# Inputs laid out transposed by the host, single first weight loads, residual steps moved, blank products first, in a two-layer decoder trunk

## The chip, the cores and the metric

The kernel runs on one core of a Trainium2 chip. The metric is device microseconds of one execution of the program on that core; lower is better. TensorE (PE in the profile) multiplies, ScalarE (ACT) and VectorE (DVE) work beside it, GpSimd (POOL) does little, and SyncE (SP) issues all DMAs.

## The reference, cut to what matters

S = 256 positions, D = 2048, two post-norm layers, float32. Layer 0 mixes tokens with a causal pooling, layer 1 with causal differential attention; in both a 4-head cross-attention into 256 memory tokens runs beside.

```python
kv = mem @ w_kv                                   # per layer: 2048 x 1024
h = x @ w_in                                      # 2048 x 2048 (pool) or 2048 x 5120 (differential)
y = jnp.concatenate([mix, mem_o], axis=-1) @ w_out[i]
x = _layernorm(DEEPNORM_ALPHA * x + y, ln1_g[i], ln1_b[i])
h = x @ w_up                                      # 2048 x 11264: gate and up halves
hc = conv_b + sum(conv_w[kk] * hp[:, kk:kk + S] for kk in range(CONV_WIDTH))
f = (jax.nn.silu(gate) * up) @ w_down             # 5632 x 2048
x = _layernorm(DEEPNORM_ALPHA * x + f, ln2_g[i], ln2_b[i])
```

## The kernel before

**Products.** Every weight matrix streams once from HBM. It is cut into chunks of 512 columns, a chunk into pieces of 512 rows (1 MB, one DMA), a piece into 4 granules of 128 rows. Each float32 operand is split into a rounded high part and the rest: ScalarE writes w_hi (`hi_granule`, L430), VectorE w_lo = raw - w_hi (`lo_granule`, L775), and TensorE makes three products, w_hi by x_hi, w_hi by x_lo and w_lo by x_hi (`product3`, L1310 to L1312). A granule is 12 products of 256 columns or 6 of 512. `raw` has four slots of one piece; SP may refill a slot once VectorE has split its piece (`slot_split`; in the differential stage, whose `tail` is set, the wait is for one piece more in three of four cases). w_hi and w_lo hold 8 granules, so ScalarE and VectorE are at most 8 granules ahead of TensorE.

**Order.** All engines run written-out programs and meet in semaphores. A position in a stage is named (n, j): piece n, granule j. The order of the stages: `s_kv` (memory keys and values of both layers, chunks 0 to 3), `s_pool_in`, `s_pool_w`, `s_out[0]`, `s_up[0]` (22 chunks in 11 pairs g: gate chunk 2g, up chunk 2g + 1), `s_down[0]`, `s_diff` (10 chunks, n = 0 to 39, with attention heads beside), `s_out[1]`, `s_up[1]`, `s_down[1]`.

**The start.** SP loads mem in token rows, interleaved with chunk 0's weights; the first piece comes as four single granules (L343). TensorE transposes mem against an identity that GpSimd makes (`ahead`, `transpose_bank`, L1373), four transposes per PSUM bank of two 128-column blocks; the first call takes banks 0 and 1. x is loaded beside chunk 1's weights and transposed in pieces n = 4 to 11 of `s_kv`, one bank per piece, between the products. `split_hi` and `split_lo` make the two parts of each bank from PSUM. After each chunk `kv_out` (L545) copies it out.

**The feed-forward pair.** While a gate chunk 2g streams (`ffn_gate`), ScalarE applies the taps of the up chunk just finished (`taps`, L529), VectorE adds the two lagging taps (`conv_bank`, L935) and multiplies with the silu. While an up chunk 2g + 1 streams (`ffn_up`), taps and silu of the gate chunk are made.

**The deferred gain and bias.** After a norm, x_tok holds the normed value without gain and bias. `resid_affine` multiplies the gain row in (L894) and adds the bias row (L897), 512 columns at a time, as a side task of the next stage. The rows lie in the one buffer `gb`. SP's `load_rows` waits until the step before has freed it, and stands in SP's program like this:

```python
with nc.sync.Fori(0, 4) as g:
    load_pair(g)              # 8 pieces: chunks 2g and 2g + 1
    load_rows(l, 0, 2 * l, g) # waits for resid_affine(g - 1, 1)
```

In pairs 1 to 4 VectorE does step (g - 1, 0) after piece 2 of the chunk 2g + 1 and step (g - 1, 1) two granules later. In the differential stage the steps for c stand at (n % 4, j) = (2, 2) and (3, 2) of the chunk after c, and `load_rows(c)` behind the four pieces of chunk c.

## Time and profile before

| | |
|---|---|
| median of three runs | 2241.58 us (2238.80 to 2241.73) |
| the profiled execution, its own time | 2234.63 us |
| its span, first to last instruction | 2232.9 us |
| TensorE busy | 97% of the span |
| mean granted clock | 0.99 |
| DMA, 10 to 20 us and 20 to 30 us | 393 and 387 GB/s |
| issue of SP's second load (the first weight granule) | 1.25 us |
| w_lo of one granule on VectorE (L775), mean | 685 ns |
| VectorE's first residual sum into x_tok (L820) | 241.02 us |

Times in rows are microseconds from the span's start. Products are pipelined: each shows a longer duration than the distance to the next, so TensorE's pace is read from starts, and a wait of TensorE is an idle time in brackets with what ended it. The clock column reads 1.00 in the first ten microseconds, where the starts of the products are what tells the clock. "L775" is line 775 of the kernel.

### The profile page before, as it was taken

The page shows a single profiled execution, that of the slowest core. Times are in us where ns is not written, and L with a number is a line of the kernel's source. Part 1 is how long each engine was busy: PE and PEld are TensorE (multiplying, and loading weights), DVE is VectorE, ACT ScalarE, POOL GpSimd, SP SyncE. Part 2 cuts the span into 40 slices and gives each one's busy share as a digit, 9 for nine tenths or more (in the row PEclk, how much of TensorE's full clock was granted, in tenths as well). Part 3 has the DMA queues.
Part 4 walks back from the last instruction along what each step waited for, and adds up shares of the span by engine and source line. Part 5 has one row for each costly group of instructions (what it writes and reads, how often), then busy time and mean ns, then how long its engine had stood idle before and what let it go on. Part 6 is the DMA issues. An engine that isn't in the chain of part 4 may idle for free.

```text
span 2232.9 us, 39246 instructions
## 1 busy us (share of the span) xinstructions
PE 2175.7 (97%) x14328; PEld 1973.4 (88%) x14328; DVE 1368.6 (61%) x2456; ACT 1124.5 (50%) x2112; POOL 9.4 (0%) x15
## 2 busy tenths in 40 slices
PE   8999999999999999999999999999999999999996
PEld 8999889999999998888777777889999999988885
DVE  5557666666756575455656557566767666665555
ACT  5545555545555454444545556465545455544442
POOL 0000000000000000000000000000000000000001
PEclk9999999999999999999999999999999999999998
DMA  8555545456555555555444454544555555465552
GB/s 312 171 177 167 200 159 180 160 171 242 183 193 182 194 173 185 188 190 187 142 170 160 151 171 154 203 161 163 200 204 175 194 175 196 153 242 207 188 188 75
DMA packets 204510, 406.65 MB, mean 182 GB/s; under 512 B 7696, under 2 KB 9744, under 8 KB 203920
## 3 DMA queue, kind: packets, MB, share of 16 engines
q1 hardware_dynamic: 204432, 405.61, 52.8%
q8 instruction: 49, 0.80, 0.1%
q14 instruction: 29, 0.24, 0.0%
HBM read 402.44 MB, written 3.15 MB: 182 GB/s over the span
## 4 chain that ended last, share of the span: by engine, by line
PE 88%; DVE 5%; DMA 3%; ACT 2%; issue 2%; SPq 0%; DVEq 0%; ACTq 0%
PE acc L1310 28%; PE acc L1311 28%; PE acc L1312 28%; DMA raw<-in_ffn_w_up 2%; DVE w_lo L775 2%; PE acc L1373 1%; ACT w_hi L430 1%; DMA raw<-in_diff_w_in 1%; DVE conv L935 1%; PE acc L1542 0%; DVE x_tok L897 0%; PE acc L1516 0%; DVE x_tok L894 0%; PE acc L1437 0%; DVE x_tok L1282 0%
## 5 line engine op out<-in xcount | busy, mean ns | idle before, releaser
L775 DVE TENSOR_TENSOR w_lo<-raw,w_hi 128x512 fp32r<-128x512 f32 x1484 | 961.0, 685 | 504.0 <-ACT w_hi L430 501.1
L430 ACT ACTIVATE w_hi<-raw 128x512 fp32r<-128x512 f32 x1480 | 864.6, 627 | 558.8 <-PE acc L1312 472.9
L1310 PE MATMUL acc<-ffn_xT,w_hi 128*128 128x256 f32 x3072 | 865.8, 282 | 11.0 <-DVE w_lo L775 10.8
L1311 PE MATMUL acc<-ffn_xT,w_hi 128*128 128x256 f32 x3072 | 862.2, 281 | 0.0
L1312 PE MATMUL acc<-ffn_xT,w_lo 128*128 128x256 f32 x3072 | 862.1, 281 | 0.0
L1310 PEld LDWEIGHTS acc<-ffn_xT,w_hi 128*128 128x128 f32 x3072 | 580.2, 189 | 13.1 <-DVE w_lo L775 12.0
L1311 PEld LDWEIGHTS acc<-ffn_xT,w_hi 128*128 128x128 f32 x3072 | 580.2, 189 | 0.2
L1312 PEld LDWEIGHTS acc<-ffn_xT,w_lo 128*128 128x128 f32 x3072 | 580.1, 189 | 0.0
L935 DVE SCALAR_TENSOR_TENSOR conv<-acc,table,conv 128x255 f32<-128x255 f32 (+1 forms) x352 | 153.3, 477 | 224.4 <-ACT conv L529 211.8
L1310 PE MATMUL acc<-w_hi,ffn_act 128*128 128x512 f32 x704 | 279.1, 397 | 0.0
L1311 PE MATMUL acc<-w_lo,ffn_act 128*128 128x512 f32 x704 | 278.4, 395 | 0.0
L1312 PE MATMUL acc<-w_hi,ffn_act 128*128 128x512 f32 x704 | 276.7, 393 | 0.0
L1310 PE MATMUL acc<-w_hi,ffn_xT 128*128 128x512 f32 x576 | 235.8, 409 | 1.6 <-DVE w_lo L775 0.8
L1312 PE MATMUL acc<-w_hi,ffn_xT 128*128 128x512 f32 x576 | 228.2, 396 | 0.0
L1311 PE MATMUL acc<-w_lo,ffn_xT 128*128 128x512 f32 x576 | 227.8, 395 | 0.0
L529 ACT ACTIVATE conv<-acc,table 128x256 f32<-128x256 f32 x176 | 84.8, 562 | 195.9 <-PE acc L1312 195.9
L1312 PEld LDWEIGHTS acc<-w_hi,ffn_act 128*128 128x128 f32 x704 | 132.2, 188 | 32.9
L1310 PEld LDWEIGHTS acc<-w_hi,ffn_act 128*128 128x128 f32 x704 | 132.1, 188 | 32.2
L1311 PEld LDWEIGHTS acc<-w_lo,ffn_act 128*128 128x128 f32 x704 | 132.1, 188 | 31.1
L1312 PEld LDWEIGHTS acc<-w_hi,ffn_xT 128*128 128x128 f32 x576 | 108.7, 189 | 27.1
L1310 PEld LDWEIGHTS acc<-w_hi,ffn_xT 128*128 128x128 f32 x576 | 109.1, 189 | 26.1 <-DVE ffn_xT L797 1.6
L1311 PEld LDWEIGHTS acc<-w_lo,ffn_xT 128*128 128x128 f32 x576 | 109.1, 189 | 23.3
(177 smaller groups left out, 1058.9 us busy)
## 6 DMA issues: line engine op xcount, KB each, us to landing
raw<-in_ffn_w_up SPq DMA_DIRECT2D x176, 1024.0 KB, 4.9
raw<-in_ffn_w_down SPq DMA_DIRECT2D x88, 1024.0 KB, 5.1
raw<-in_diff_w_in SPq DMA_DIRECT2D x40, 1024.0 KB, 5.5
raw<-in_w_out SPq DMA_DIRECT2D x32, 1024.0 KB, 5.1
raw<-in_pool_w_in SPq DMA_DIRECT2D x16, 1024.0 KB, 5.2
raw<-in_mem_w_kv SPq DMA_DIRECT2D x15, 1024.0 KB, 8.8
gb<-in_ln_g SPq DMA_DIRECT2D x12, 256.0 KB, 4.3
gb<-in_ln_b SPq DMA_DIRECT2D x12, 256.0 KB, 6.3
```

The lines of the kernel that those rows point to most:

```text
L430: nc.scalar.activation(w_hi[:, st.split_at(k, j), 0:st.width], raw[:, k % SLOTS, j * CHUNK:j * CHUNK + st.width], ACT.Copy).then_inc(hi_ma ...
L529: ins = nc.scalar.activation(conv[:, s, b, f * S:(f + 1) * S], acc[:, 2 * s + b, f * S:(f + 1) * S], ACT.Identity, bias=table[:, l, bass.d ...
L775: nc.vector.tensor_tensor(w_lo[:, at, 0:st.width], raw[:, k % SLOTS, j * CHUNK:j * CHUNK + st.width], w_hi[:, at, 0:st.width].bitcast(F32) ...
L935: ins = nc.vector.scalar_tensor_tensor(to, acc[:, 2 * s + b, f * S:(f + 1) * S - lag], table[:, l, bass.ds(col, 1)], to, ALU.mult, ALU.add)
L1310: pe.matmul(out, w[0], x[0], start=start, stop=False, skip_group_check=True)
L1311: pe.matmul(out, w[0], x[1], start=False, stop=False, skip_group_check=True)
L1312: return pe.matmul(out, w[1], x[0], start=False, stop=stop, skip_group_check=True)
L1373: ins = pe.transpose(acc[:, b, f * S + t * P:f * S + (t + 1) * P], src[:, t, (kt + f) * P:(kt + f + 1) * P], ident[:, :])
```

## The change

The host passes x and mem also as x_T and mem_T, 128 rows of [16 blocks, 256 positions]. SP loads mem_T in seven parts (`MEM_PARTS`: 1, 1, 2, 2, 2, 4, 4 blocks) between the weights of chunk 0, whose first two pieces come as eight single granules with a semaphore each; x_T comes in four parts beside chunk 1. ScalarE and VectorE split both from SBUF (`mem_hi`, `x_hi`, `mem_lo`, `x_lo`), x in pieces 8 to 15 of `s_kv` and no longer 4 to 12; TensorE's 16 banks of transposes go. x_tok is still needed later and gets a 2 MB load of its own behind the memory weights of layer 1. VectorE clears a tile, and TensorE makes eight blank 128-column products of it at the very start. The residual steps move: in the feed-forward pairs from the last two pieces of chunk 2g + 1 to piece 1 of the gate chunk 2g; in the differential stage one piece earlier, and there `load_rows(c)` now stands ahead of piece 3 of chunk c.

```diff
+MEM_PARTS = ((0, 1), (1, 2), (2, 4), (4, 6), (6, 8), (8, 12), (12, 16))
+SINGLES = 2 * PIECE
...
-        return (c * self.uses[s] + (self.loads[s] + k // SLOTS + 1)) * 16
+        return (c * self.uses[s] + (self.loads[s] + k // SLOTS + 1) - (1 if s < SINGLES // PIECE else 0)) * 16
...
-        for c, (name, to, loaded) in enumerate((("mem", mem_tok, mem_loaded), ("x", x_tok, x_loaded))):
-            src = a[name][0].rearrange("(t p) n -> p t n", p=P)
-            for k in range(4):
-                cs = slice(k * CHUNK, (k + 1) * CHUNK)
-                if c > 0 or k > 0:
-                    sp.dma_start(to[:, :, cs], src[:, :, cs]).then_inc(loaded[k], 16)
-                    load_piece(s_kv, c, k, a["mem_w_kv"][0], c * CHUNK)
-                    continue
-
-                half = CHUNK // 2
-                sp.dma_start(to[:, :, 0:half], src[:, :, 0:half]).then_inc(mem_half_loaded, 16)
-                for j in range(PIECE):
-                    sp.dma_start(raw[:, 0, j * CHUNK:(j + 1) * CHUNK], a["mem_w_kv"][0][j * P:(j + 1) * P, 0:CHUNK]).then_inc(
-                        granule_loaded[j] if j < PIECE - 1 else piece_loaded[0], 16)
-                    if j == 0:
-                        sp.dma_start(to[:, :, half:CHUNK], src[:, :, half:CHUNK]).then_inc(loaded[0], 16)
+        def load_mem(i):
+            lo, hi = MEM_PARTS[i]
+            sp.dma_start(mem_raw[:, lo:hi, :], a["mem_T"][:, lo:hi, :]).then_inc(mem_loaded[i], 16)
+
+        def load_single(i):
+            j = i % PIECE
+            sp.dma_start(raw[:, i // PIECE, j * CHUNK:(j + 1) * CHUNK], a["mem_w_kv"][0][i * P:(i + 1) * P, 0:CHUNK]).then_inc(
+                granule_loaded[i], 16)
+
+        for i in range(SINGLES):
+            if i in (0, 1, 2, 4, 6):
+                load_mem((0, 1, 2, 4, 6).index(i))
+            load_single(i)
+        for k in range(2, 4):
+            load_mem(3 + k)
+            load_piece(s_kv, 0, k, a["mem_w_kv"][0], 0)
+        for k in range(4):
+            load_piece(s_kv, 1, k, a["mem_w_kv"][0], CHUNK)
+            sp.dma_start(x_raw[:, 4 * k:4 * k + 4, :], a["x_T"][:, 4 * k:4 * k + 4, :]).then_inc(x_loaded[k], 16)
...
+        sp.dma_start(x_tok[:, :, :], a["x"][0].rearrange("(t p) n -> p t n", p=P)).then_inc(x_tok_loaded, 16)
...
-                    load_chunk(s_diff, c, a["diff_w_in"][0], DIFF_ORDER[c] * CHUNK, OUT_PIECES[1] if c == DIFF_LAST else None)
+                    for k in range(4):
+                        load_piece(s_diff, c, k, a["diff_w_in"][0], DIFF_ORDER[c] * CHUNK, OUT_PIECES[1][k] if c == DIFF_LAST else None)
+                        if k == 2 and c < 4:
+                            load_rows(0, 1, 1, c)
                     if c == 0:
                         sp.wait_ge(kv1_stored, 16)
                         sp.wait_ge(granule_used, s_down[0].used(3))
                         sp.dma_start(kv1[:, :, :], kv1_dram[:, :, :]).then_inc(kv1_loaded, 16)
-                    if c < 4:
-                        load_rows(0, 1, 1, c)
...
+        def mem_hi(lo, hi):
+            for part, loaded in zip(MEM_PARTS, mem_loaded):
+                if part[0] == lo:
+                    act_e.wait_ge(loaded, 16)
+            nc.scalar.activation(memT[:, lo:hi, 0, :], mem_raw[:, lo:hi, :], ACT.Copy).then_inc(hi_split["mem"], 1)
+
+        def x_hi(b):
+            if b % 2 == 0:
+                act_e.wait_ge(x_loaded[b // 2], 16)
+            nc.scalar.activation(xT[:, 2 * b:2 * b + 2, 0, :], x_raw[:, 2 * b:2 * b + 2, :], ACT.Copy).then_inc(hi_split["x"], 1)
+
+        for n in range(16):
             c, k = n // 4, n % 4
             for j in range(PIECE):
-                hi_granule(s_kv, c, k, j)
-                if c == 0 and j in (0, 2):
-                    b = 2 * k + j // 2
-                    split_hi("mem", b, memT, 2 * b, acc[:, 4 + b % 4, :])
-                if 5 <= n < 13 and j == 1:
-                    split_hi("x", n - 5, xT, 2 * (n - 5), acc[:, 4 + (n - 5) % 4, :])
+                i = PIECE * n + j
+                if i < 2:
+                    mem_hi(i, i + 1)
+                elif i < KT and i % 2 == 0:
+                    mem_hi(i, i + 2)
+                if i < SINGLES:
+
+                    act_e.wait_ge(granule_loaded[i], 16)
+                    nc.scalar.activation(w_hi[:, s_kv.split_at(k, j), :], raw[:, k, j * CHUNK:(j + 1) * CHUNK], ACT.Copy).then_inc(hi_made, 1)
+                else:
+                    hi_granule(s_kv, c, k, j)
+                if 8 <= n and j == 1:
+                    x_hi(n - 8)
...
+        nc.vector.memset(conv[:, 0, 0, 0:P], 0.0).then_inc(blank_made, 1)
...
+        def mem_lo(lo, hi):
+            dve.wait_ge(hi_split["mem"], lo + 1 if lo < 2 else lo // 2 + 2)
+            nc.vector.tensor_tensor(memT[:, lo:hi, 1, :], mem_raw[:, lo:hi, :], memT[:, lo:hi, 0, :].bitcast(F32),
+                                    ALU.subtract).then_inc(split["mem"], 1)
+
+        def x_lo(b):
+            dve.wait_ge(hi_split["x"], b + 1)
+            kts = slice(2 * b, 2 * b + 2)
+            nc.vector.tensor_tensor(xT[:, kts, 1, :], x_raw[:, kts, :], xT[:, kts, 0, :].bitcast(F32), ALU.subtract).then_inc(split["x"], 1)
+
+        for n in range(16):
             c, k = n // 4, n % 4
             for j in range(PIECE):
+                i = PIECE * n + j
+                if i < 2:
+                    mem_lo(i, i + 1)
+                elif i < KT and i % 2 == 0:
+                    mem_lo(i, i + 2)
                 lo_granule(s_kv, c, k, j)
-                if c == 0 and j in (0, 2):
-                    b = 2 * k + j // 2
-                    split_lo("mem", b, memT, 2 * b, acc[:, 4 + b % 4, :])
-                if 5 <= n < 13 and j == 1:
-                    split_lo("x", n - 5, xT, 2 * (n - 5), acc[:, 4 + (n - 5) % 4, :])
+                if 8 <= n and j == 1:
+                    x_lo(n - 8)
...
+                dve.wait_ge(x_tok_loaded, 16)
...
-                    if c < 4 and n % 4 >= 2 and j == 2:
-                        resid_affine(0, 1, 1, c, n % 2)
+                    if c < 4 and n % 4 in (1, 2) and j == 2:
+                        resid_affine(0, 1, 1, c, n % 4 - 1)
...
-            def ffn_gate(g):
+            def ffn_gate(g, resid):
                 lo_piece(s_up[l], 2 * g, 0)
                 conv_bank(l, 1, 0, g - 1)
-                lo_piece(s_up[l], 2 * g, 1)
+                lo_granule(s_up[l], 2 * g, 1, 0)
+                if resid:
+                    resid_affine(l, 0, 2 * l, g - 1, 0)
+                lo_granule(s_up[l], 2 * g, 1, 1)
+                lo_granule(s_up[l], 2 * g, 1, 2)
+                if resid:
+                    resid_affine(l, 0, 2 * l, g - 1, 1)
+                lo_granule(s_up[l], 2 * g, 1, 3)
                 conv_bank(l, 1, 1, g - 1)
                 product(l, 0, g - 1)
                 lo_piece(s_up[l], 2 * g, 2)
@@ -1239,24 +1275,17 @@
                 lo_piece(s_up[l], 2 * g, 3)
                 act_lo_part(l, 1, g - 1)
 
-            def ffn_up(g, resid=False):
+            def ffn_up(g):
                 lo_piece(s_up[l], 2 * g + 1, 0)
                 conv_bank(l, 0, 0, g)
                 lo_piece(s_up[l], 2 * g + 1, 1)
                 conv_bank(l, 0, 1, g)
                 lo_piece(s_up[l], 2 * g + 1, 2)
-                if resid:
-                    resid_affine(l, 0, 2 * l, g - 1, 0)
-                lo_granule(s_up[l], 2 * g + 1, 3, 0)
-                lo_granule(s_up[l], 2 * g + 1, 3, 1)
-                if resid:
-                    resid_affine(l, 0, 2 * l, g - 1, 1)
-                lo_granule(s_up[l], 2 * g + 1, 3, 2)
-                lo_granule(s_up[l], 2 * g + 1, 3, 3)
+                lo_piece(s_up[l], 2 * g + 1, 3)
 
             def ffn_pair(g, resid):
-                ffn_gate(g)
-                ffn_up(g, resid)
+                ffn_gate(g, resid)
+                ffn_up(g)
...
-        pe.wait_ge(ident_made, 2)
+        pe.wait_ge(blank_made, 1)
+        for _ in range(8):
+            pe.matmul(acc[:, 7, 0:P], conv[:, 0, 0, 0:P], conv[:, 0, 0, 0:P], start=True, stop=True)
 
         for n in range(16):
             c, k = n // 4, n % 4
             if c >= 2 and k == 0:
                 pe.wait_ge(kv_evacuated, c - 1)
-            if 4 <= n < 12:
-                b = n - 4
-                pe.wait_ge(x_loaded[b // 2], 16)
-                if b < 4:
-                    pe.wait_ge(split["mem"], 5 + b)
-                else:
-                    pe.wait_ge(split["x"], b - 3)
-                transpose_bank("x", b, 4 + b % 4, x_tok, 2 * b)
             for j in range(PIECE):
-                if c == 0 and j % 2 == 0:
-                    ahead("mem", 2 * k + j // 2, mem_tok, lambda b: pe.wait_ge(mem_loaded[b // 2] if b > 0 else mem_half_loaded, 16))
+                i = PIECE * n + j
+                if i < 2:
+                    pe.wait_ge(split["mem"], i + 1)
+                elif i < KT and i % 2 == 0:
+                    pe.wait_ge(split["mem"], i // 2 + 2)
...
+    for name in ("x", "mem"):
+        laid_out[f"{name}_T"] = np.asarray(inputs[name])[0].reshape(S, KT, P).transpose(2, 1, 0)
```

## Rows read from the trace of the kernel before

**Rows 1.** The page's chain that ended last: share of each engine
```profile
PE 88%; DVE 5%; DMA 3%; ACT 2%; issue 2%; SPq 0%; DVEq 0%; ACTq 0%
```

**Rows 2.** Timeline of ScalarE, chunk copies: start us, us, engine line; idle before, releaser
```profile
34.21 1.02 ACT L545 ACTIVATE memory_kv<-acc 128x1024 f32<-128x1024 f32 x1 [5.00 <-PE acc L1312]
...
58.38 1.03 ACT L545 ACTIVATE memory_kv<-acc 128x1024 f32<-128x1024 f32 x1 [3.97 <-PE acc L1312]
...
83.06 1.03 ACT L545 ACTIVATE memory_kv<-acc 128x1024 f32<-128x1024 f32 x1 [4.06 <-PE acc L1312]
...
105.46 1.03 ACT L545 ACTIVATE memory_kv<-acc 128x1024 f32<-128x1024 f32 x1 [4.97 <-PE acc L1312]
```

**Rows 3.** Timeline of TensorE, the first products
```profile
7.64 0.56 PE L1310 MATMUL acc<-memory_memT,w_hi 128*128 128x256 f32 x1
8.00 0.42 PE L1311 MATMUL acc<-memory_memT,w_hi 128*128 128x256 f32 x1
8.21 0.41 PE L1312 MATMUL acc<-memory_memT,w_lo 128*128 128x256 f32 x1
...
9.68 0.28 PE L1310 MATMUL acc<-memory_memT,w_hi 128*128 128x256 f32 x1
```

**Rows 4.** Chain that ended last, first 140 us: start us, us, what
```profile
1.76 5.06 DMA memory_mem<-in_mem
...
34.17 0.44 PE acc L1373 x4
```

**Rows 5.** One source line: the single first weight loads, L343
```profile
DMA to landing us min/median/max: 4.1/5.3/5.5
```

**Rows 6.** TensorE's waits, 390-560, then 1535-1660 us: total, times, longest
```profile
PE acc L1310 <- DVE w_lo L775: 5.5, 3, 1.8
...
PE acc L1310 <- DVE w_lo L775: 5.3, 3, 2.0
```

**Rows 7.** Timeline of ScalarE: taps, first work after a feed-forward chunk's end
```profile
387.06 1.47 ACT L529 ACTIVATE conv<-acc,table 128x256 f32<-128x256 f32 x3 [5.29 <-PE acc L1312]
...
532.29 1.02 ACT L529 ACTIVATE conv<-acc,table 128x256 f32<-128x256 f32 x2 [5.21 <-PE acc L1312]
...
577.35 1.48 ACT L529 ACTIVATE conv<-acc,table 128x256 f32<-128x256 f32 x3 [5.21 <-PE acc L1312]
...
1533.28 1.47 ACT L529 ACTIVATE conv<-acc,table 128x256 f32<-128x256 f32 x3 [5.21 <-PE acc L1312]
...
1675.60 1.93 ACT L529 ACTIVATE conv<-acc,table 128x256 f32<-128x256 f32 x4 [5.21 <-PE acc L1312]
```

**Rows 8.** Chain that ended last, 300-830 us, around the first stall
```profile
399.05 1.17 DVE x_tok L897
...
401.77 8.14 DMA raw<-in_ffn_w_up
```

**Rows 9.** Windows: busy of each engine, PEclk (granted), DMA share, GB/s
```profile
508.00:510.00 2.00, 2.00 (x11) 2.00 (x11) 1.90 (x5) 2.00 (x5) 0.00 (x0) 0.50 1.05 384
```

**Rows 10.** Timeline of VectorE, one gate chunk and one up chunk
```profile
372.16 2.69 DVE L775 TENSOR_TENSOR w_lo<-raw,w_hi 128x512 fp32r<-128x512 f32 x4
...
396.65 1.21 DVE L894 TENSOR_TENSOR x_tok<-x_tok,gb 128x1024 f32 x1
397.79 1.28 DVE L775 TENSOR_TENSOR w_lo<-raw,w_hi 128x512 fp32r<-128x512 f32 x2
```

**Rows 11.** Timeline of TensorE, first product of that gate's ninth granule
```profile
375.24 0.28 PE L1310 MATMUL acc<-ffn_xT,w_hi 128*128 128x256 f32 x1
```

**Rows 12.** Timeline of TensorE, its three waits in the differential projection
```profile
1129.79 0.50 PE L1310 MATMUL acc<-w_hi,ffn_xT 128*128 128x512 f32 x1 [0.79 <-DVE w_lo L775]
...
1162.06 1.22 PE L1437 MATMUL acc<-diff_probs,diff_kv 128*128 128x256 f32 x2 [4.47 <-ACT diff_probs L494]
...
1193.85 0.39 PE L1542 MATMUL acc<-diff_qkT 64*128 64x128 f32 x2 [1.00 <-ACT diff_scores L655]
```

**Rows 13.** Timeline of VectorE, the residual add before the longest of them
```profile
1149.21 1.22 DVE L897 TENSOR_TENSOR x_tok<-x_tok,gb 128x1024 f32<-128x1024 f32 x1
```

More of the change, by code:

```diff
@@ L208, in build @@
     xT, act = region("ffn", [split_x, ("act", [P, FF_T, 2, S], F32R)])
-    _, kvbuf, qmT0, memT, mem_tok = region("memory", [
+    _, kvbuf, qmT0, memT, mem_raw, x_raw = region("memory", [
         split_x, ("kv", [P, 8, 512], F32), ("qmT", [P, MEM_HEADS, S], F32), ("memT", [P, KT, 2, S], F32R),
-        ("mem", [P, TT, D], F32)])
+        ("mem", [P, KT, S], F32), ("x", [P, KT, S], F32)])
     _, _, _, dT, pool_h, pool_a, pool_b, probs0 = region("pool", [
@@ L250, in build @@
     s_out, s_up, s_down = (s_out0, s_out1), (s_up0, s_up1), (s_down0, s_down1)
-    mem_half_loaded, granule_loaded = sem("mem_half_loaded"), [sem(f"granule_loaded{j}") for j in range(PIECE - 1)]
+    granule_loaded = [sem(f"granule_loaded{i}") for i in range(SINGLES)]
     piece_loaded = [sem(f"piece_loaded{s}") for s in range(SLOTS)]
@@ L256, in build @@
     granule_used = sem("granule_used")
-    x_loaded = [sem(f"x_loaded{c}") for c in range(4)]
-    mem_loaded = [sem(f"mem_loaded{c}") for c in range(4)]
+    mem_loaded = [sem(f"mem_loaded{i}") for i in range(len(MEM_PARTS))]
+    x_loaded, x_tok_loaded = [sem(f"x_loaded{i}") for i in range(4)], sem("x_tok_loaded")
     table_loaded, small_loaded = sem("table_loaded"), sem("small_loaded")
     zeroed, ident_made, steps_made, pads_made = sem("zeroed"), sem("ident_made"), sem("steps_made"), sem("pads_made")
-    rounded = sem("rounded")
+    rounded, blank_made = sem("rounded"), sem("blank_made")
     pool_evacuated, pool_diffed, dT_hi, dT_made = sem("pool_evacuated"), sem("pool_diffed"), sem("dT_hi"), sem("dT_made")
@@ L993, in sine_arguments @@
             nc.vector.tensor_scalar(trig[:, 2, :, :], part, -1.0, math.pi / 2, ALU.mult, ALU.add).then_inc(trig_arg, 1)
-        split_lo("mem", 0, memT, 0, acc[:, 4, :])
-        lo_granule(s_kv, 0, 0, 0)
-        split_lo("mem", 1, memT, 2, acc[:, 5, :])
-        for j in range(1, PIECE):
-            lo_granule(s_kv, 0, 0, j)
-        for n in range(1, 16):
+        def mem_lo(lo, hi):
[7 more added lines that the diff above has]
+        for n in range(16):
             c, k = n // 4, n % 4
             for j in range(PIECE):
-                lo_granule(s_kv, c, k, j)
-                if c == 0 and j in (0, 2):
-                    b = 2 * k + j // 2
-                    split_lo("mem", b, memT, 2 * b, acc[:, 4 + b % 4, :])
-                if 5 <= n < 13 and j == 1:
-                    split_lo("x", n - 5, xT, 2 * (n - 5), acc[:, 4 + (n - 5) % 4, :])
+                i = PIECE * n + j
[3 more added lines that the diff above has]
+                    mem_lo(i, i + 2)
+                lo_granule(s_kv, c, k, j)
+                if 8 <= n and j == 1:
+                    x_lo(n - 8)
                 if (n, j) == (13, 3):
@@ L1374, in transpose_bank @@
             ins.then_inc(banked[stage], 1)
-        def ahead(stage, i, src, need):
-            for b in ((0, 1), (2, 3))[i] if i < 2 else (i + 2,):
-                if b < KT // 2:
-                    need(b)
-                    if b >= 4:
-                        pe.wait_ge(split[stage], b - 3)
-                    transpose_bank(stage, b, 4 + b % 4, src, 2 * b)
-            pe.wait_ge(split[stage], i + 1)
         def normed_ahead(l, n, kt):
@@ L1410, in mem_beside @@
                         if l == 0:
+                            pe.wait_ge(ident_made, 2)
                             pe.wait_ge(qm_evacuated, 1)
@@ L1628, in build @@
     ctx.close()
-_INS = ["table", "x", "mem", "positions", "pool_w_in", "pool_w", "diff_w_in", "diff_lambda_q1", "diff_lambda_k1",
+_INS = ["table", "x", "x_T", "mem_T", "positions", "pool_w_in", "pool_w", "diff_w_in", "diff_lambda_q1", "diff_lambda_k1",
         "diff_lambda_q2", "diff_lambda_k2", "diff_subln_g", "mem_w_kv", "w_out", "ln1_g", "ln1_b", "ffn_w_up",
```

7 lines of the change are left out of this document (removed).

## The prediction

> **What bounds the kernel now.** I began with the chain that ended last: TensorE holds 88% of it [rows 1]. So only two things shorten this kernel: less TensorE work, or fewer stretches in which it stands still or runs at half clock. The work itself has a floor that can be read off: ScalarE copies each finished chunk of the first projection out, and chunks 2 to 3 ended 105.46 - 83.06 = 22.40 us apart [rows 2]. That is 16 granules (a granule is one 128-row slab of weights) at 1.40 us. In the feed-forward network one pair of chunks without a gap takes 577.35 - 532.29 = 45.06 us [rows 7]. Every stage is held against these figures; what is above them is what a change can give back.
>
> Three places stand above the floor where the diff works. **The start:** chunk 0 ends at 34.21 instead of 22.4 us after the first product, and chunks 1 and 2 take 24.17 and 24.68 [rows 2]. **The feed-forward pairs 1 to 4:** TensorE waits three times in each layer for w_lo, 5.5 and 5.3 us in sum [rows 6]. **The memory and score part of the differential projection:** three waits of 0.79, 4.47 and 1.00 us [rows 12].
>
> The feed-forward waits have one cause, to be read backwards in the chain [rows 8]: TensorE waits for w_lo, that for a weight load of 8.14 us, and that was issued late because SP stood at `load_rows`, which waits for the residual add L897. SP issues in order. It asks for gain row g right after pair g's last piece, while VectorE sends the signal only in the last piece of that pair; the slots of the next chunk are long free, but nobody fills them.
>
> **The change, part by part.**
>
> 1. *Transposes out.* x needs 8 banks, mem 8 banks, four transposes each, 0.44 us on TensorE's path per bank [rows 4]. The x banks sit four in chunk 1 and four in chunk 2: 4 x 0.44 = 1.76 us each, which is just chunk 1's 24.17 - 22.40 = 1.77. Sum 3.5 us. The copies on ScalarE and VectorE stay, with an SBUF source; same size, taken at the same price, and hidden by the several granules that these engines are ahead there.
>
> 2. *The first chunk.* Now the first product starts at 7.64 [rows 3], because the second mem load landed only at 1.76 + 5.06 = 6.82 [rows 4] and its transposes stood in TensorE's queue ahead of it. Afterwards granule 0 needs a 128 KB mem part and one 256 KB weight load. The single weight loads landed 4.1 to 5.5 us after issue [rows 5]; issued second, at 1.25 as before (the table), that is 5.35, and less if the smaller load ahead helps; plus a split of about 0.6 and 0.7 on the two engines: 6.3 to 6.8. So 0.8 to 1.3 us earlier. Chunk 0 then took 34.0 - 7.64 = 26.4 us. Over 22.4 that is 4.0: the six later mem banks (6 x 0.44 = 2.6) and the products at half clock. Those start 0.21 apart instead of 0.117 (22.40 / 192) until 9.68 [rows 3], about 1 us lost. I keep that 1 us. Against it: can the loads keep up? Chunk 0 needs 6 MB for mem and weights. At the 390 GB/s of the table the last 1 MB piece is in after about 21 us, and granule 12, which needs it, is due at about 24; piece 2 (granule 8) is in at about 17 to 18 and due at 18 to 19. It is tight there, so I charge 0.7. Chunk 0 ends at 6.5 + 22.4 + 1.0 + 0.7 = 30.6: 3.4 to 3.6 us earlier (bounds: 2 if granules 1 to 8 come one by one late, 5 if the half clock goes too). With part 1: 7.1 us.
>
> The blank products fill TensorE before any data is there. The row shows that before, the full rate came at 9.68, after the transposes and two us of products. The Trainium skill ("TensorE: Matmul & The Clock Gate", Part 1) says that activity releases the clock, so the blanks might bring that forward. By the rule the start would be worth up to 1 us more, but the loads bound the same stretch, so by the row it is nothing; I take nothing.
>
> 3. *x_tok loaded a second time.* 2 MB on SP's queue behind the second layer's memory weights: some 5.4 us of transfer at 390 GB/s, once, while three pieces (3 x 5.6 us of TensorE) are ahead. VectorE first sums into it at 241 us (the table), during the output projection. Nothing.
>
> 4. *Feed-forward: residual steps to the gate chunk's second piece.* The signal for gain row g now comes in pair g's piece 1, before SP has issued the pair's last piece, so `load_rows` finds it there and the three stalls of each layer go. What they cost: from chunk 3's start to chunk 9's TensorE takes 532.29 - 387.06 = 145.23 us in layer 0, 10.05 above 3 x 45.06; in layer 1 1675.60 - 1533.28 = 142.32, 7.14 above [rows 7]. That holds the waits and what followed (the clock fell to 0.50 behind one, [rows 9]). Gain 17.2 us.
>  What it costs: two instructions, which hold VectorE 397.79 - 396.65 = 1.14 us [rows 10], two 2.28 us, now in piece 1 of the gate chunk; the tightest granule behind them is the first of piece 2. Its w_lo begins at 372.16 [rows 10], takes 0.69 (the page's mean, 685 ns), and TensorE uses it at 375.24 [rows 11]: 2.39 us to spare. The move eats 2.28. It fits by a hair, at eight gates; I charge 0.1 us in all (bounds: 0, and 8 x 1 us if the conv steps beside it stretch). Behind it the products, `act_lo` and the up chunk have more room.
>
> 5. *Differential projection: residual one piece earlier, gain rows before piece 3.* This looks like the same cure and isn't. SP asks for row c ahead of piece 3 of chunk c; the signal comes in piece 2 of the same chunk. So SP still stands until VectorE is there, and then it is piece 3, not the next chunk's piece 0, which is late, with the same two granules and the same lead to cover some 8 us of load. Stall one: before 0.79; after, by the same sum, about 1. Stall two: VectorE ended L897 at 1149.21 + 1.22 = 1150.4 [rows 13]; TensorE ran dry 7.2 us later (1162.06 - 4.47 = 1157.6) and resumed at 1162.06 [rows 12], 11.6 after L897: gain rows asked for, 8 us of load, the copies and the head's exp behind it on ScalarE. After, the same 11.6 us hits the head before it, and L894 now runs in that head's stretch on VectorE, so the 7.2 shrink by up to 1.14: 4.5 to 5.6 us. Stall three: piece 3 lands before the first scores, saves up to 1.0. And the multiply L894 now stands at VectorE between head maxima that TensorE waits for: up to 1.14. Sum 0.8 us slower (bounds: 8 us faster if the lead does cover the load, as below; 6 slower if a stall doubles).
>
> **Sum**, against the profiled execution's own 2234.63 us (span 2232.9 and 1.7 around it): -7.1 - 17.2 + 0.8 + 0.1 = -23.4, so 2211.2. The median of the plain runs is 2241.58, 7 us above that execution, so the forecast for the median is 2241.6 - 23.4 = 2218.2; 2218.
>
> **The rivals**, in the median's terms.
>
> A. *The start is bound by its loads.* The first eight weight loads are 256 KB, each with its own way to landing; if they feed TensorE more slowly than 1.4 us a granule, the removed transposes turn into waits for w_lo in chunk 0, and only 3.5 + 0.5 us of part 1 and 2 are left: 2221. For it: even 256 KB took 4.1 to 5.5 us [rows 5]. Against: they overlap. The Trainium skill ("DMA: Bandwidth & Descriptors", Rules for kernel authors) asks for 1 MiB or more per load for full bandwidth; this rival is what that rule would do here. Chance 0.13.
>
> B. *The differential stage gets clearly worse.* Piece 3's late load meets the memory head chain with less lead and a second stretch at half clock: 6 us more, 2224. For it: one such wait already cost 4.47 [rows 12]. Chance 0.15.
>
> C. *The differential stage is relieved.* VectorE reaches piece 2 when TensorE is still nine granules behind (12.6 us), so the load is covered: 0.79 + 4.47 + 1.00 = 6.3 go, and half clock behind the long one, an estimate of 2 from [rows 9], which shows 1.0 lost in 2 us; with my 0.8 that is 9 us: 2209. Chance 0.12.
>
> D. *The feed-forward stalls stay*, because SP still reaches `load_rows` before the signal: then only the start is won, 2235. Against: between the two places lie some six pieces of VectorE's work. Chance 0.03.
>
> E. *Slower.* The one mechanism is the gate: the 2.28 us lie where TensorE's chunk end, the taps and the conv steps run in series. Were nothing to spare, each of eight gates would lose 2.28 us and, as in [rows 9], 1.0 of half clock: 26 us, 2244. It decides from 23.5 / 8 = 2.9 us per gate on. Against: 2.39 to spare [rows 10, 11]. Chance 0.03.
>
> My forecast holds 0.54. Range 2210 to 2228: it takes in A and B with their neighbours and the 5-us bound of the start, and leaves C's core, D and E outside. Some 0.2 % (4.5 us) is what a measurement of this kernel can tell from no change; faster by more 0.95, within it 0.02, slower 0.03.
>
> **What would show it.** The chunk copies (now L545) at about 30.8, 53.2, 75.6 and 98.0; no wait of TensorE for w_lo in the pairs 1 to 4 and even chunks of 22.5 us; SP's `load_rows` no longer followed by loads issued in a burst there, but still so in the differential stage, with one long TensorE wait near a memory head. Waits for w_lo at each gate's ninth granule would speak for E. The forecast fails if the stalls of the pairs reappear elsewhere, above all in the differential stage, where the sum rests on leads of a few us.

## The result and the profile after

The changed kernel takes 2216.67 us (median of 4 runs, 2215.53 to 2217.42), the kernel before, beside it on the same chip, 2240.19 us (4 runs, 2237.16 to 2241.73). The ratio is 0.9896, with a 95% interval of 0.9879 to 0.9913: 23.5 us faster. The forecast was 2218.0. The profiled execution after took 2216.79 us (span 2215.0), 17.8 less than the profiled one of before; e1 and e9 below bear on why the two differences are unequal.

The page's chain, share of each engine, answers [rows 1]: less DVE and DMA, so less of the end hangs on late weights.

```profile
PE 92%; DVE 4%; DMA 2%; ACT 1%; issue 1%; SPq 0%; DVEq 0%; ACTq 0%
```

ScalarE's timeline, the chunk copies and then the taps, answers [rows 2] and [rows 7].

```profile
30.63 1.03 ACT L554 ACTIVATE memory_kv<-acc 128x1024 f32<-128x1024 f32 x1 [3.38 <-PE acc L1341]
53.02 1.02 ACT L554 ACTIVATE memory_kv<-acc 128x1024 f32<-128x1024 f32 x1 [4.96 <-PE acc L1341]
75.80 1.03 ACT L554 ACTIVATE memory_kv<-acc 128x1024 f32<-128x1024 f32 x1 [5.06 <-PE acc L1341]
98.20 1.02 ACT L554 ACTIVATE memory_kv<-acc 128x1024 f32<-128x1024 f32 x1 [4.96 <-PE acc L1341]
...
380.52 1.93 ACT L538 ACTIVATE conv<-acc,table 128x256 f32<-128x256 f32 x4 [5.28 <-PE acc L1341]
...
516.35 1.93 ACT L538 ACTIVATE conv<-acc,table 128x256 f32<-128x256 f32 x4 [5.21 <-PE acc L1341]
...
1521.46 1.93 ACT L538 ACTIVATE conv<-acc,table 128x256 f32<-128x256 f32 x4 [5.21 <-PE acc L1341]
...
1657.81 1.94 ACT L538 ACTIVATE conv<-acc,table 128x256 f32<-128x256 f32 x4 [5.21 <-PE acc L1341]
```

The four copies stand within 0.2 us of the forecast 30.8, 53.2, 75.6 and 98.0. By the last one the start gave 105.46 - 98.20 = 7.3 us. The same six chunks of the feed-forward network take 516.35 - 380.52 = 135.83 and 1657.81 - 1521.46 = 136.35 us, where [rows 7] gave 145.23 and 142.32: 15.4 us less. Three pairs without a gap would be 135.2.

TensorE's timeline, four stretches: the start, the gate's ninth granule, and the differential projection. It answers [rows 3], [rows 11] and [rows 12].

```profile
5.82 0.36 PE L1339 MATMUL acc<-memory_memT,w_hi 128*128 128x256 f32 x1 [1.16 <-DVE w_lo L795]
6.02 0.28 PE L1340 MATMUL acc<-memory_memT,w_hi 128*128 128x256 f32 x1
6.14 0.28 PE L1341 MATMUL acc<-memory_memT,w_lo 128*128 128x256 f32 x1
...
8.02 0.36 PE L1339 MATMUL acc<-memory_memT,w_hi 128*128 128x256 f32 x1 [0.54 <-DVE w_lo L795]
...
9.90 0.36 PE L1339 MATMUL acc<-memory_memT,w_hi 128*128 128x256 f32 x1 [0.21 <-DVE w_lo L795]
...
18.96 0.35 PE L1339 MATMUL acc<-memory_memT,w_hi 128*128 128x256 f32 x1 [0.36 <-DVE w_lo L795]
...
368.43 0.28 PE L1341 MATMUL acc<-ffn_xT,w_lo 128*128 128x256 f32 x1
368.61 0.39 PE L1339 MATMUL acc<-ffn_xT,w_hi 128*128 128x256 f32 x1
...
1109.38 0.50 PE L1339 MATMUL acc<-w_hi,ffn_xT 128*128 128x512 f32 x1 [2.59 <-DVE w_lo L795]
...
1142.64 2.07 PE L1457 MATMUL acc<-diff_probs,diff_kv 128*128 128x256 f32 x4 [5.67 <-ACT diff_probs L503]
```

Three things are to be seen. The first product starts at 5.82 instead of 7.64, and from the second on they are 0.12 apart: full rate from the start, in this execution; under e8 are others. Granules 0, 1, 2 and 8 of chunk 0 now wait for their weights. And two waits of the differential projection grew: 0.79 became 2.59, 4.47 became 5.67; the third, of 1.00, is gone.

VectorE's timeline in that gate chunk, with both residual steps (L914, L917), and then the residual steps of the differential projection, answers [rows 10] and [rows 13].

```profile
361.38 1.22 DVE L914 TENSOR_TENSOR x_tok<-x_tok,gb 128x1024 f32 x1
...
363.72 1.22 DVE L917 TENSOR_TENSOR x_tok<-x_tok,gb 128x1024 f32 x1
...
367.86 2.69 DVE L795 TENSOR_TENSOR w_lo<-raw,w_hi 128x512 fp32r<-128x512 f32 x4
...
1096.09 1.22 DVE L917 TENSOR_TENSOR x_tok<-x_tok,gb 128x1024 f32<-128x1024 f32 x1
...
1129.37 1.22 DVE L917 TENSOR_TENSOR x_tok<-x_tok,gb 128x1024 f32<-128x1024 f32 x1
```

The ninth granule's w_lo begins at 367.86 and is ready 0.69 later, at 368.55; TensorE takes it at 368.61, 0.18 after the product ahead of it where the pace is 0.12. The slack of 2.39 us is used up to nothing, and the product comes 0.06 us late. Over all eight gates the distances around the ninth granule add up to 0.8 us above the pace.

SP's timeline in the differential projection: both gain-row loads (L333), then weights.

```profile
1097.34 0.34 SPq L333 DMA_DIRECT2D gb<-in_ln_g  x1
1097.72 0.43 SPq L333 DMA_DIRECT2D gb<-in_ln_b  x1
1098.20 13.33 SPq L323 DMA_DIRECT2D raw<-in_diff_w_in  x4
...
1130.61 0.34 SPq L333 DMA_DIRECT2D gb<-in_ln_g  x1
1131.00 0.43 SPq L333 DMA_DIRECT2D gb<-in_ln_b  x1
1131.47 13.67 SPq L323 DMA_DIRECT2D raw<-in_diff_w_in  x4
```

Both times the rows are asked for right as L917 ends (1096.09 + 1.22 = 1097.31, 1129.37 + 1.22 = 1130.59): SP had stood there. The chain of the same stretch gives the loads behind them:

```profile
1098.20 9.75 DMA raw<-in_diff_w_in
...
1131.47 8.27 DMA raw<-in_diff_w_in
```

### The profile page after: what moved, and what is told of

Read it like the earlier page. It is cut to its first block, busy times and chain, and to the rows that moved or that the text cites. A ratio compares the mean times of both kernels' runs of the same rounds, so it can differ in the third digit from the quotient of the medians.

```text
span 2215.0 us, 39167 instructions
## 1 busy us (share of the span) xinstructions
PE 2169.3 (98%) x14280; PEld 1967.5 (89%) x14280; DVE 1371.5 (62%) x2458; ACT 1127.3 (51%) x2113; POOL 9.4 (0%) x15
## 4 chain that ended last, share of the span: by engine, by line
PE 92%; DVE 4%; DMA 2%; ACT 1%; issue 1%; SPq 0%; DVEq 0%; ACTq 0%
PE acc L1339 30%; PE acc L1341 30%; PE acc L1340 30%; DVE w_lo L795 1%; DMA raw<-in_diff_w_in 1%; PE acc L1402 1%; DMA raw<-in_mem_w_kv 0%; ACT w_hi L439 0%; PE acc L1533 0%; PE acc L1559 0%; DVE x_tok L1311 0%; PE acc L1457 0%; DVE stats L859 0%; DVE x_tok L858 0%; PE acc L1563 0%
## 5 line engine op out<-in xcount | busy, mean ns | idle before, releaser
L439 ACT ACTIVATE w_hi<-raw 128x512 fp32r<-128x512 f32 (+1 forms) x1476 | 862.5, 627 | 502.3 <-PE acc L1341 472.1
## 6 DMA issues: line engine op xcount, KB each, us to landing
raw<-in_mem_w_kv SPq DMA_DIRECT2D x14, 1024.0 KB, 10.6
```

The costliest lines, as they stand in the source:

```text
L439: nc.scalar.activation(w_hi[:, st.split_at(k, j), 0:st.width], raw[:, k % SLOTS, j * CHUNK:j * CHUNK + st.width], ACT.Copy).then_inc(hi_ma ...
```

## The experiments

Each was timed with the kernel before beside it on the same chip; each ratio is to that.

**e1. The kernel before, profiled and timed once more**, with no edit.

> The kernel before, unchanged, profiled a second time. Its first profiled execution took 2234.63 us, 5.6 us under its median of 2240.19, while the changed kernel's took 2216.79, 0.1 over its median. Theory (clock): the stalls of the old kernel sometimes cost an extra stretch at half clock and sometimes not, depending on where in time they fall; then this trace shows the same waits of TensorE within 0.2 us each, but other stretches at a clock of 0.50, and its time lies 3 to 7 us above the first profiled one. Rival (waits): the waits themselves are longer in other executions; then the waits for w_lo in the feed-forward pairs sum to well over 5.5 and 5.3 us.

Measured: 2237.06 us, ratio 0.9999 (0.9984 to 1.0013). The waits are there again (its table of waits):

```profile
PE acc L1310 <- DVE w_lo L775: 11.6, 7, 2.1
...
PE acc L1437 <- ACT diff_probs L494: 4.6, 1, 4.6
```

But the half clock behind the feed-forward stalls is not. One window of this run, then one of the profile of before, each around the end of the first stall (the number behind the five engines' is the granted clock, then come DMA share and GB/s):

```profile
410.00:418.00 8.00, 7.58 (x64) 7.58 (x65) 7.60 (x16) 6.14 (x13) 0.00 (x0) 1.00 1.03 373
```

```profile
412.00:416.00 4.00, 4.00 (x23) 4.00 (x22) 3.75 (x8) 4.00 (x10) 0.00 (x0) 0.57 1.05 386
```

The taps at 386.10 and 528.47 put layer 0's six chunks at 142.37 us here against 145.23 in [rows 7]. So some 3 us of the 17.2 that the forecast read off one execution were clock stretches that come in some executions and not in others. How long TensorE waited does not decide it: in layer 0 the three waits were 1.84, 1.81 and 1.80 us in the profile of before, with half clock behind the first and the last, and 2.06, 2.06 and 1.52 us here, with none. Yet this profiled execution took 2237.35 us, 2.7 more than the first; that is the slower pace of some chunks, told under e6 and e9.

**e2. The feed-forward part alone** in the kernel before: the residual steps in piece 1 of the gate chunk.

> Only the feed-forward part of the change on the kernel before. Theory of the prediction: SP's wait at the gain rows goes, and with it three stalls a layer; by chunk starts the two traces differ by 9.4 us in layer 0 and 5.8 us in layer 1, so the trace shows 15 us; the plain runs 15 to 21 us, if the clock stretches behind the stalls are more frequent than in the profiled execution. Rival (gate): the move is paid by waits at the ninth granule of the gate chunks; then each of the eight gates shows more than 0.3 us. Rival (start): most of the 23.5 us comes from the start; then this is under 12 us.

Measured: 2223.71 us, ratio 0.9937 (0.9922 to 0.9952), which is 14.1 us (10.7 to 17.5), a little below the 15 to 21 expected. No stall for w_lo of the kind of [rows 6] is left. The feed-forward step is most of the gain.

**e3. The start alone**: inputs transposed by the host, single loads, blanks.

> Only the start of the change (inputs laid out transposed, eight single weight loads, blank products) on the kernel before; feed-forward and differential stage as before. Theory: 7.2 us faster, constant over the executions (7 to 8), since no stall there is left to chance. Rival: over 12 us, if the missing 5.7 us between the medians and the two profiles come from the start.

Measured: 2228.84 us, ratio 0.9957 (0.9940 to 0.9974): 9.6 us (5.8 to 13.4). In the trace TensorE begins the first product of `s_pool_in` 7.0 us earlier, and the feed-forward stalls stand as before (5.4 us in three waits in layer 0). Here the first products ran at half clock in spite of the blanks (e8).

**e4. The differential part alone**: residual steps one piece earlier, `load_rows` ahead of piece 3.

> Only the differential stage's part: residual steps one piece earlier, gain rows asked for ahead of piece 3. Prediction: 0.8 us slower; by the two traces 3.7 us slower (chunks 1 and 2 together +4.9, chunks 3 and 4 -1.4). Theory: the wait for the gain rows is only moved ahead of piece 3; 2 to 5 us slower than before. Rival: the loss in the trace is the clock's chance and the part is neutral, within 1 us of before.

Measured: 2237.34 us over 12 runs, ratio 1.0003 (0.9992 to 1.0013): nothing, at most 3 us either way. TensorE's timeline has the two waits again, 0.73 and 5.28:

```profile
1124.54 0.50 PE L1311 MATMUL acc<-w_hi,ffn_xT 128*128 128x512 f32 x1 [0.73 <-DVE w_lo L776]
...
1155.86 2.07 PE L1438 MATMUL acc<-diff_probs,diff_kv 128*128 128x256 f32 x4 [5.28 <-ACT diff_probs L495]
```

**e7. The changed kernel with before's differential projection.**

> The changed kernel with the differential stage as in the kernel before. By the traces of the changed kernel and the one before that part costs 3.7 us; the part alone on the kernel before was within 1 us of it in the plain runs and 1.3 us slower in its trace. Theory: 1 to 4 us faster than the changed kernel. Rival: no difference, under 0.5 us, the 3.7 us being chance of the clock.

Measured: 2216.84 us, ratio 0.9903 (0.9886 to 0.9921), beside 0.9896 for the whole change. So in neither surrounding can the runs tell this part from nothing. From the first product of that stage to the first of its sixth chunk TensorE took 144.40 us here, 148.97 in the trace of the whole change, 145.30 before and 145.60 in e4; the 3.7 that the profile after lost there are not what the plain runs lose. Two more traces have the same edit in that stage: 144.96 us in e8 and 147.35 in e12. So one edit gives 145.0 to 149.0 us, and what the kernel before has there gives 144.4 to 146.0 in seven traces.

**e5. The rows asked for a chunk later.** In the changed kernel, the differential residual steps go back to where they were, and SP asks for the rows of c behind piece 2 of chunk c + 1:

```diff
-                        if k == 2 and c < 4:
-                            load_rows(0, 1, 1, c)
+                        if k == 2 and 1 <= c < 5:
+                            load_rows(0, 1, 1, c - 1)
...
-                    if c < 4 and n % 4 in (1, 2) and j == 2:
-                        resid_affine(0, 1, 1, c, n % 4 - 1)
+                    if c < 4 and n % 4 >= 2 and j == 2:
+                        resid_affine(0, 1, 1, c, n % 2)
```

> The changed kernel, but in the differential stage the residual steps stand where they stood before, and SP asks for gain row c only behind piece 2 of chunk c + 1, by which time VectorE's signal is there. Theory: what is lost in that stage is SP standing still in front of free slots; then TensorE's waits of 2.6 (w_lo in chunk 1), 5.7 (the memory head) and about 1 us (chunk 3) go and so do the two half-clock stretches of 3.4 and 6.8 us behind the first two (1.7 and 3.4 us): chunks 0 to 4 of the stage take 135 to 139 us instead of 149, and the kernel is 10 to 14 us faster than the changed one. Rival: the head chains set the pace there anyway; then under 4 us.

Measured: 2206.29 us, ratio 0.9847 (0.9831 to 0.9863); its median is 10.4 us below the changed kernel's. From e7 it differs in SP's request alone, and it is 10.6 us below e7, timed on the same chip beside the same runs of before; the two intervals are far apart. From the first product of the stage to that of its sixth chunk TensorE took 135.16 us, as the theory had it. One window of 95 us over the stage's first four chunks, this kernel first, the changed kernel below it:

```profile
1085.00:1180.00 95.00, 95.00 (x450) 76.44 (x449) 57.65 (x117) 50.13 (x110) 0.00 (x0) 1.00 0.54 177
```

```profile
1095.00:1190.00 95.00, 86.74 (x394) 69.03 (x392) 48.47 (x103) 42.88 (x97) 0.00 (x0) 0.95 0.48 161
```

TensorE is busy all 95 us at full clock, where the changed kernel leaves 8.3 idle and has 0.95 of the clock. Together with e7 this shows the cause that the forecast named: where SP's request stands relative to VectorE's signal.

**e10. The feed-forward stalls cured on SP's side alone.** In the kernel before, the residual steps unmoved:

```diff
-            with nc.sync.Fori(0, 4) as g:
-                load_pair(g)
-                load_rows(l, 0, 2 * l, g)
+            load_pair(0)
+            with nc.sync.Fori(1, 5) as g:
+                load_chunk(s_up[l], 2 * g, a["ffn_w_up"][l], g * CHUNK)
+                load_rows(l, 0, 2 * l, g - 1)
+                load_chunk(s_up[l], 2 * g + 1, a["ffn_w_up"][l], g * CHUNK + D_FF)
```

> The kernel before, with one edit: in the feed-forward stage SP issues the gain and skip rows of the next gate pair one gate chunk later; the residual steps themselves stay where they were. Theory that SP's waiting behind the residual step is the whole cause of the feed-forward stalls: all of e2's gain, 14 us (2223 to 2226 us, ratio 0.9925 to 0.995), with no wait of the ninth piece in the gate chunks. Rival (VectorE's place of the residual step counts for itself): under half of it, 2231 us or more, and the stalls of 4 to 6 us behind each gate pair stay in the trace.

Measured: 2217.46 us, ratio 0.9921 (0.9900 to 0.9941): 17.7 us (13.2 to 22.3), all of e2's; the intervals overlap. The excess need not be the edit's: no chunk of this trace runs at the slower pace told below, 34 of e2's do, and 34 x 0.26 = 8.7 us is most of the 9.7 by which the two profiled executions differ. The one wait for w_lo left in the whole run (its table of waits) is in the differential projection:

```profile
PE acc L1312 <- DVE w_lo L777: 0.9, 1, 0.9
```

No product at a gate's ninth granule is late either. SP's waiting is the whole cause of those stalls; VectorE's place plays no part of its own, and the gate need not be touched.

**e6 and e9. Both stages together**: e5, and the feed-forward residual steps in and behind the gate chunk's piece 3; SP's feed-forward request stays where it was. e9 is the same kernel again.

> As the run before it, and in the feed-forward pairs the two residual steps stand in and behind piece 3 of the gate chunk instead of in piece 1. Theory: the short waits at the ninth granule of eight gate chunks (0.05 to 0.15 us each in the changed kernel's trace) go; 0.5 to 1.2 us in sum. A second theory, from the traces of this study: products of 256 columns run in one of two paces, 22.53 or 22.78 us a feed-forward chunk, and the pace is taken anew at a wait of TensorE; then with no wait in a feed-forward stage all 21 chunks of a layer have the same pace, fast or slow. Rival: the pace changes in mid-stage without a wait.

> The kernel of e6 once more, unchanged, to look again at its trace. Theory of the two paces: its time is 2199.9 us plus 5.5 us for each layer's up-projection (21 chunks of 256-column products) that runs at the slow pace. A profile near 2199.9 has none of the 42 chunks slow, one near 2205.4 has 21, one near 2211 has all 42, and the mean of a chunk is 22.53 or 22.78 us with hardly anything between. Rival (the spread comes from transfers or from the clock): a profile near 2205.4 has its 5.5 us in stalls or in a stretch at half clock, with as few slow chunks as that of e6. Ratio to the kernel before 0.985 either way.

Measured: 2205.48 us, ratio 0.9848 (0.9830 to 0.9865), and 2200.34 us, ratio 0.9843 (0.9820 to 0.9866). The nine runs lie in two groups, five at 2199.73 to 2200.59 and four at 2205.44 to 2205.90, with nothing between. Both profiles were of the lower group, so the waits and the pace of an upper one were not seen. What a pace is, two timelines of ScalarE show, this kernel's (e9) and e8's, taps four chunks apart in a stretch in which TensorE is never idle:

```profile
559.16 1.93 ACT L538 ACTIVATE conv<-acc,table 128x256 f32<-128x256 f32 x4 [5.21 <-PE acc L1341]
...
649.26 1.93 ACT L538 ACTIVATE conv<-acc,table 128x256 f32<-128x256 f32 x4 [5.21 <-PE acc L1341]
```

```profile
563.15 1.93 ACT L538 ACTIVATE conv<-acc,table 128x256 f32<-128x256 f32 x4 [5.27 <-PE acc L1340]
...
654.28 1.93 ACT L538 ACTIVATE conv<-acc,table 128x256 f32<-128x256 f32 x4 [5.27 <-PE acc L1340]
```

That is 90.10 against 91.13 us for four chunks (768 products), 0.26 a chunk. Windows of both over 560 to 650 us read busy throughout and the same granted clock:

```profile
560.00:650.00 90.00, 90.00 (x769) 90.00 (x768) 58.31 (x104) 47.78 (x89) 0.00 (x0) 1.00 0.56 186
```

```profile
560.00:650.00 90.00, 90.00 (x761) 90.00 (x760) 58.38 (x104) 47.89 (x88) 0.00 (x0) 1.00 0.56 185
```

The 21 chunks of one layer after the first would be 21 x 0.255 = 5.4 us, the distance of the two groups. This fits and is not shown for them. For the two profiled executions of before the traces have it: in the six chunks with the stalls e1 took 2.9 us less in layer 0 and 0.4 less in layer 1, and among the other chunks it had 26 slow ones against 2, 24 x 0.255 = 6.1 us more (an estimate). The sum, 2.8, is near the 2.7 between them.

**e8. The changed kernel without the blanks.**

> The changed kernel without the blank products. In its trace the first real products start 0.12 us apart, at full clock, where those of the kernel before started 0.21 apart until 9.68 us. Theory (the prediction's): the loads bound the first granules (TensorE waits for w_lo at granules 1, 2 and 8), so the half clock is hidden and this is under 0.7 us slower. Rival (clock rule): the blanks bring the clock up, and without them 1 to 2 us are lost, chunk 0 ending at 31.5 or later instead of 30.4.

Measured: 2220.37 us, ratio 0.9903 (0.9886 to 0.9920), not told apart from the changed kernel's by the runs. TensorE's timeline has the first product at 5.81 and starts 0.21 apart until 11.50:

```profile
6.38 0.41 PE L1340 MATMUL acc<-memory_memT,w_lo 128*128 128x256 f32 x1
6.59 0.41 PE L1338 MATMUL acc<-memory_memT,w_hi 128*128 128x256 f32 x1
```

Chunk 1's first product comes at 31.20, 0.77 us later than in the profile after. That is not the price of the blanks, for the traces with the same start and the same blanks differ among themselves. The products were 0.12 apart from the second on in the profile after, e5 and e12; they were 0.21 apart until 10.35 in e3, 9.12 in e6, 9.70 in e7 and 9.10 in e9. TensorE's timeline of e9:

```profile
5.77 0.55 PE L1339 MATMUL acc<-memory_memT,w_hi 128*128 128x256 f32 x1 [0.93 <-DVE w_lo L795]
6.13 0.42 PE L1340 MATMUL acc<-memory_memT,w_hi 128*128 128x256 f32 x1
6.34 0.41 PE L1341 MATMUL acc<-memory_memT,w_lo 128*128 128x256 f32 x1
```

Chunk 1 began at 30.43 and 30.37 in the profile after and e5 (full rate), and at 30.65, 30.46, 31.18 and 30.75 in e3, e6, e7 and e9 (half clock). So half clock at the start costs 0 to 0.8 us here, and whether the blanks save any of it is not shown; in e8, without them, it lasted longest.

**e11. The blanks alone** in the kernel before.

> The kernel before with the eight blank matmuls put ahead and nothing else. Theory (the blanks warm the clock for the first products and do no more): 0.5 to 1.2 us faster, ratio 0.9995, the first products 0.12 us apart from their start at about 7.6 us, where before they were 0.21 to 0.23 apart; as the loads bound this chunk's end too, up to half of it may be lost again in waits for pieces. Rival (the blanks delay the first transposes or the weight load): first product at 8 us or later and no gain. The interval of the ratio will hold 1 either way, so the trace decides.

Measured: 2235.14 us over 12 runs, ratio 0.9991 (0.9976 to 1.0007), and in its trace the theory does not hold. TensorE's timeline from the end of the blanks, which run from 1.06 us:

```profile
4.63 1.06 PE L1374 MATMUL acc<-ident,memory_mem 128*128 128x128 f32 x4
6.42 1.12 PE L1374 MATMUL acc<-ident,memory_mem 128*128 128x128 f32 x4 [0.72 <-DMA memory_mem<-in_mem]
7.80 0.55 PE L1311 MATMUL acc<-memory_memT,w_hi 128*128 128x256 f32 x1 [0.26 <-DVE w_lo L775]
...
9.64 0.41 PE L1313 MATMUL acc<-memory_memT,w_lo 128*128 128x256 f32 x1
9.86 0.31 PE L1311 MATMUL acc<-memory_memT,w_hi 128*128 128x256 f32 x1
```

The first products are 0.21 apart until 9.86, later than the 9.68 of [rows 3]. In this execution the blanks brought nothing. The transposes and 0.98 us of idle time between them and the first product need not be the reason: with no work in between, four of the seven traces under e8 had half clock too. What decides is open.

**e12. Four single loads instead of eight** in the changed kernel, with the mem parts of blocks 4 to 7 ahead of the 1 MB piece 1:

```diff
-SINGLES = 2 * PIECE
+SINGLES = PIECE
...
-            if i in (0, 1, 2, 4, 6):
-                load_mem((0, 1, 2, 4, 6).index(i))
+            if i in (0, 1, 2):
+                load_mem((0, 1, 2).index(i))
...
+        load_mem(3)
+        load_mem(4)
+        load_piece(s_kv, 0, 1, a["mem_w_kv"][0], 0)
```

> The changed kernel, with the first four weight pieces alone loaded one by one as now but the rest of chunk 0 and the memory tokens' last two parts in another order: the memory parts go ahead of the 1 MB piece 1. Theory (the start is bound by the bytes that must land before the last product of chunk 0, whatever their order): chunk 1 starts within 0.5 us of the changed kernel's 30.43 us and the ratio stays at 0.9896. Rival (the order of these loads holds the start back): chunk 1 starts 1 us or more away from it, earlier if the memory parts were late, later if the pieces were.

Measured: 2219.93 us, ratio 0.9926 (0.9906 to 0.9947). TensorE starts as early, but the next piece's first granule is 2.50 us late, and chunk 1 begins 2.7 us later:

```profile
15.97 0.36 PE L1342 MATMUL acc<-memory_memT,w_hi 128*128 128x256 f32 x1 [2.50 <-DVE w_lo L798]
```

My theory, that only the sum of the bytes counts, fell: how soon the second piece's first granule lands counts. Size and order of the loads were changed together, so the 2.7 us are the price of both, and neither has been priced alone.

## Why the prediction was right, term by term

**Start, -7.1.** It held: 7.3 in the profile, and 7.0 in e3's. Inside, a pair of errors cancelled. The forecast kept 1 us of half clock and charged 0.7 for the loads. In the profile after the half clock was gone, and in its place came waits for weights, 0.54 + 0.21 + 0.36 = 1.1 us behind the first product. (The 1.16 before it is no loss against the forecast: it came at 5.82, ahead of the 6.3 to 6.8.) In e3 the half clock stayed and TensorE waited for no weights in chunk 0, and chunk 1 began 0.2 us later. So the forecast's reason for taking nothing for the blanks, that the loads bound the same stretch, was right. The Trainium skill ("TensorE: Matmul & The Clock Gate", Part 1) says that activity releases the clock; of the seven traces with this start and the blanks, three agree at the first product and four show full rate only at 9.1 to 10.4 us. Part 1's 3.5 is in the copies, 22.39 and 22.78 apart. The single loads landed in

```profile
DMA to landing us min/median/max: 3.1/6.0/6.6
```

against [rows 5]; that granules of 256 KB come one after the other just ahead of TensorE is rival A's mechanism at a small price. The Trainium skill ("DMA: Bandwidth & Descriptors", Rules for kernel authors) asks for 1 MiB or more per load for full bandwidth. e12 puts a 1 MB load where four singles stood and loses 2.7 us; at a start, where the first landing counts, that speaks against the rule, though the order of the loads was changed with it.

**x_tok's second load, nothing.** No wait for it; the waits for transposes behind the norms are 13.7 us in three before and after.

**Feed-forward, -17.2 and +0.1.** The mechanism was right and the size too large: 15.4 in the profiles, 14.1 alone (10.7 to 17.5). Two parts of the excess can be read. Some 3 us of the 145.23 were clock stretches that e1 had not. And 135.83 + 136.35 is 1.8 above the 270.4 of six gapless pairs. Of that 0.4 is the gates in them, where the slack forecast at a hair was a hair short (0.8 over all eight gates): the 0.1 for all eight was too small but right in kind, and rival E, which needed 2.9 us a gate to decide, was far. The rest of the 1.8 is the slower pace of single chunks, told below.

**Differential projection, +0.8.** The reading that this is not the same cure was right. Stall two was put at 4.5 to 5.6 and measured 5.67, and 5.28 and 5.54 in e4 and e8; stall three went. Stall one was put at 1 and measured 2.59 in the profile after, 2.27 in e12, 0.73 in e4 and 1.13 in e8, the same edit each time. It goes with the load behind the rows, which took 9.75, 9.44, 7.90 and 8.29 us in these four, where the forecast had some 8; in the two long cases TensorE's clock also halved behind the wait. This is the step that failed in size, and what made the load longer is open. In plain runs the part costs nothing that can be told from zero (e4, e7), so neither rival B nor C is seen. C's saving was real, but it needed another edit, e5's: 9 us forecast there, 10.4 measured. That SP still stands because it asks before the signal, the forecast's argument, is what e5 turned round.

**From one execution to the median.** The sum, -23.4 from a profiled execution, met -23.5 between medians, while the profiles differ by only 17.8. The parts alone give 14.1 + 9.6 - 0.7 = 23.0, with intervals of several us each. In the profile the terms are -7.3, -15.4 and +3.7, and the remaining +1.2 is clock stretches and pace. The execution of before that was profiled had the slower pace in only 2 of its chunks without a stall (9 of 42 with the stalled ones, by the distances of the products) and lay 7 us under the median that the forecast started from; that of e1 had it in 26 (32 of 42). That median is uncertain too: the four sets of runs of the kernel before have medians of 2240.19, 2237.41, 2239.42 and 2234.43. So part of the agreement to 1 us is luck: the feed-forward term was too large by 2 to 3 us, the start alone gave more than 7.1 in the plain runs' middle value, and which of pace and clock made up the rest was not settled.

## What to carry to other kernels

An in-order queue must not be asked for something whose release comes later than the queue's own next duty. Count, in pieces, how far the signal lies ahead of the request, on either side: moving the request later (e10) was worth no less than moving the signaller earlier (e2), cost no slack on VectorE, and helped where moving both one piece had not (e5 against e4). The best version measured is that of e6 and e9, with the differential request a chunk later and the feed-forward residual steps in the gate's last piece: 2200 to 2206 us, ratios 0.9848 and 0.9843. e10's later request together with e5's was not run.

## What the runs showed of the hardware

Products of 256 columns run at one of two paces with TensorE never idle and the granted clock at 1.00: 90.10 or 91.13 us for four chunks, 117.3 or 118.7 ns a product. From the second feed-forward chunk of a layer on, in all fourteen traces, the pace changed only where TensorE takes up weights that come late, at a stall or at a gate chunk's ninth granule (there the product was late by 0.1 us, or by as little as 0.01), and kept until the next such place; what sets it is open. Over 42 chunks it is up to 10.7 us, against a spread of 14.3 us of the kernel before in one set of 17 runs (2230.32 to 2244.65). By their length, stalled chunks left out, 2 chunks were slow in the profile of before, 26 in e1, 34 in e2, 6 after and none in e6, e9 and e10. Which pace follows a wait looks like chance; fewer waits only mean fewer draws.

Half clock behind a short wait comes in some executions and not in others: in one execution of the kernel before it stood at 412 and 508 us, behind two of the six feed-forward stalls of 1.6 to 2.0 us, in another behind none of the six, and in e11 again behind two. Half clock at the start does too: with the same start and the same blanks the first products ran at full rate in three traces and at half clock in four (e8). So what the clock costs cannot be read off one trace.
